# Input transposes ahead of the first modulation quarter, constant matmuls in TensorE's queue, and a low part behind the gating of the second channel half

## The reference

```python
mod_l = (silu(c) @ w_mod + b_mod)[:, None, :]          # w_mod: 1024 x 6144
sh1_l, s1_l, g1_l, sh2_l, s2_l, g2_l = jnp.split(mod_l, 6, axis=-1)
hl = modulate(rms_norm(xl, norm1_g), sh1_l, s1_l)      # h * (1 + scale) + shift
u = hl @ w_pw1 + b_pw1                                 # 1024 -> 2048
a, gate = jnp.split(u, 2, axis=-1)
u = a * jax.nn.sigmoid(gate)
u = dwconv(u.reshape(B * n_seg, L // n_seg, D), w_dw).reshape(B, L, D) + b_dw
u = jax.nn.silu(layer_norm(u, ln_g, ln_b))
yl = u @ w_pw2 + b_pw2
xl = xl + g1_l * yl
```

## Time and profile before

| | us |
|---|---|
| median of 3 runs (lowest, highest) | 1057.15 (1057.11, 1057.98) |
| the profiled execution | 1056.59 |
| its span | 1054.8 |
| TensorE busy | 1009.1 |
| VectorE busy | 604.5 |
| ScalarE busy | 512.8 |
| GpSimd busy | 24.2 |

### The profile page before, as it was taken

One profiled execution on the slowest core, in us unless ns is written; L12 is line 12 of the kernel. 1 busy time (PEld: TensorE's weight loads), 2 busy tenths in 40 slices (PEclk: granted clock), 3 DMA queues, 4 the chain that ended last, 5 costly groups with the idle time before them and its releaser, 6 DMA issues.

```text
span 1054.8 us, 13782 instructions
## 1 busy us (share of the span) xinstructions
PE 1009.1 (96%) x5788; PEld 854.1 (81%) x5788; DVE 604.5 (57%) x691; ACT 512.8 (49%) x643; POOL 24.2 (2%) x47
## 2 busy tenths in 40 slices
PE   5998999999998999899999999999998999999996
PEld 3665779999987999787888888889987788888885
DVE  3487455443558658756555545664886554554464
ACT  4444456445444547644443444654664544434453
POOL 0000000000000000000000000000000100000000
PEclk8999999999999999999999999999999999999998
DMA  9967587555515533055555555435322555555531
GB/s 353 410 232 278 234 348 274 202 189 195 192 51 204 183 142 121 2 180 204 203 185 180 194 199 204 164 133 190 121 80 81 190 199 196 176 186 199 179 121 40
DMA packets 30647, 195.56 MB, mean 185 GB/s; under 512 B 3571, under 2 KB 5672, under 8 KB 9592
## 3 DMA queue, kind: packets, MB, share of 16 engines
q1 hardware_dynamic: 30586, 194.68, 51.1%
HBM read 193.61 MB, written 2.04 MB: 185 GB/s over the span
## 4 chain that ended last, share of the span: by engine, by line
PE 80%; DVE 11%; ACT 4%; issue 3%; DMA 1%; POOL 0%; SPq 0%; DVEq 0%; POOLq 0%; ACTq 0%
PE ps L1527 56%; PE ps L1885 9%; PE ps L1938 4%; DVE lo L1006 3%; ACT hi L569 2%; PE ps L1623 2%; DVE scratch L1328 1%; DVE scratch L1144 1%; DMA raw<-stream 1%; PE ps L2164 1%; PE ps L2068 1%; PE ps L2022 1%; PE ps L2141 1%; PE ps L1640 1%; PE ps L1604 1%
## 5 line engine op out<-in xcount | busy, mean ns | idle before, releaser
L1006 DVE TENSOR_TENSOR lo<-raw,hi 128x2048 fp32r<-128x2048 f32 (+4 forms) x140 | 316.0, 2260 | 255.1 <-ACT hi L569 255.0
L569 ACT ACTIVATE hi<-raw 128x2048 fp32r<-128x2048 f32 (+4 forms) x140 | 263.9, 1888 | 135.7 <-PE ps L1527 114.7
L1527 PE MATMUL ps<-hi,xh 128*128 128x512 f32 (+2 forms) x704 | 275.3, 391 | 10.5 <-DVE lo L1006 5.8
L1527 PE MATMUL ps<-lo,xh 128*128 128x512 f32 (+2 forms) x704 | 269.1, 382 | 0.0
L1527 PE MATMUL ps<-hi,xl 128*128 128x512 f32 (+2 forms) x704 | 269.1, 382 | 0.0
L1527 PEld LDWEIGHTS ps<-hi,xh 128*128 128x128 f32 x704 | 132.3, 188 | 46.3 <-issue 12.6
L1527 PEld LDWEIGHTS ps<-lo,xh 128*128 128x128 f32 x704 | 132.3, 188 | 25.1
L1527 PEld LDWEIGHTS ps<-hi,xl 128*128 128x128 f32 x704 | 132.5, 188 | 22.6
L1527 PE MATMUL ps<-hi,gh 128*128 128x512 f32 (+2 forms) x328 | 125.1, 382 | 0.0
L1527 PE MATMUL ps<-lo,gh 128*128 128x512 f32 (+2 forms) x328 | 124.6, 380 | 0.0
L1527 PE MATMUL ps<-hi,gl 128*128 128x512 f32 (+2 forms) x328 | 124.6, 380 | 0.0
(11 more groups left out here) (251 smaller groups left out, 1083.1 us busy)
## 6 DMA issues: line engine op xcount, KB each, us to landing
raw<-stream SPq DMA_DIRECT2D x142, 1024.0 KB, 4.9
scratch<-stream SPq DMA_DIRECT2D x22, 1024.0 KB, 6.4
raw<-stream SPq DMA_DIRECT2D x4, 1020.0 KB, 4.9
raw<-stream SPq DMA_DIRECT2D x4, 896.0 KB, 5.0
raw<-stream SPq DMA_DIRECT2D x2, 864.0 KB, 5.1
raw<-stream SPq DMA_DIRECT2D x2, 768.0 KB, 4.6
raw<-stream SPq DMA_DIRECT2D x2, 680.0 KB, 5.2
h<-x SPq DMA_DIRECT2D x2, 512.0 KB, 4.2
```

What stands on the lines that cost most here:

```text
L569: nc.scalar.activation(hi[:, u["s"] % SPLIT_SLOTS, 0:n], raw_of(u, n), ACT.Copy).then_inc(S["hi_done"], 1)
L1006: nc.vector.tensor_tensor(lo[:, slot, 0:n], raw_of(u, n), hi[:, slot, 0:n].bitcast(F32), ALU.subtract).then_inc(S["lo_done"], 1)
L1527: ins = nc.tensor.matmul(out, l, r, start=start and i == 0, stop=stop and i == 2, skip_group_check=skip)
```

## The change

Three edits.

On TensorE the transposes of the input come first, then quarter 0, the bias products of pw1, then quarter 1 and the column sums; before, quarter 0 stood ahead of the transposes, and quarter 1 and the column sums ahead of the bias products. ScalarE follows: both copies to `xnT`, then the copy of quarter 0.

`keep_busy(times)` multiplies `neg_ones` by itself into bank 7, which nothing reads until it is overwritten: 14 times at the very start, behind `init_p` 3, and 7 times between the bias products and quarter 1 (`WARM`).

On VectorE the low part of pw2's second unit moves from ahead of `gated(1)` to behind the normalisation of block 1.

```diff
--- before.py
+++ after.py
@@ -174,6 +174,9 @@
 COLUMN_UNITS = ((0, 1), (2, 3), (4, 5), (6, 7), (12, 13), (14, 15), (16, 17), (18, 19))
 
 
+WARM = (14, 7)
+
+
 def copies(m):
 
     return m + 1 if m < SPLIT_ROWS[0] else m + 1 - len(SPLIT_ROWS)
@@ -653,11 +656,11 @@
                     nc.scalar.activation(sig[:, b, :], ps[:, 4 * c + 2 * b + 1, :], ACT.Sigmoid).then_inc(S["sig_done"], 1)
 
             squares(0)
-            quarter_copy(0)
             for b in range(NB):
                 act.wait_ge(S["xnT_ps"], b + 1)
                 nc.scalar.activation(xnT[:, :, b * P:(b + 1) * P], ps[:, 2 * b:2 * b + 2, :].rearrange("p a (k m) -> p (a k) m", k=4),
                                      ACT.Copy).then_inc(S["xnT_ready"], 1)
+            quarter_copy(0)
             feed(units_of(("pw1", 0))[0], 0)
             quarter_copy(1)
             group_high(0)
@@ -1160,7 +1163,6 @@
             dve.wait_ge(S["in_consts"], 32)
             for dst, c in ((ident16[:], C_ID), (masks16[:, 0, :], C_CAUSAL), (masks16[:, 1, :], C_STRICT)):
                 nc.vector.tensor_copy(dst, table[:, c:c + P]).then_inc(S["masks_done"], 1)
-            feed(units_of("pw2")[1], 0)
             gated(1)
             filtered(1, 0, 1, 2, 3)
             statistics(1, 0)
@@ -1173,6 +1175,7 @@
             dve.wait_ge(S["ln_rstd"], 2)
             nc.vector.tensor_scalar(xs[:, 1, :], ps[:, 2:4, :].rearrange("p a c -> p (a c)"), ln_mv[:, 1, 0:1], ln_rstd[:, 1:2],
                                     ALU.subtract, ALU.mult).then_inc(S["xc_ready1"], 1)
+            feed(units_of("pw2")[1], 0)
             columns(4)
 
             def low_pair(i, high, low):
@@ -1714,19 +1717,27 @@
                     ins = nc.tensor.transpose(ps[:, 4 + 2 * b + k // 4, (k % 4) * P:(k % 4 + 1) * P], xs[:, b, k * P:(k + 1) * P], ident)
                 ins.then_inc(S["xcT_ps"], 1)
 
-            pe.wait_ge(S["csb_done"], 1)
-            quarters(0)
+            def keep_busy(times):
+
+                for _ in range(times):
+                    nc.tensor.matmul(ps[:, 7, 0:P], neg_ones[:], neg_ones[:], start=True, stop=True)
+
+            pe.wait_ge(S["init_p"], 3)
+            keep_busy(WARM[0])
             pe.wait_ge(S["in_ident"], 16)
             for b in range(NB):
                 pe.wait_ge(S["xs_ready"], xsval(0, b))
                 for k in range(KT):
                     ins = nc.tensor.transpose(ps[:, 2 * b + k // 4, (k % 4) * P:(k % 4 + 1) * P], xs[:, b, k * P:(k + 1) * P], ident)
                 ins.then_inc(S["xnT_ps"], 1)
-            quarters(1)
-            column_sums(0)
+            pe.wait_ge(S["csb_done"], 1)
+            quarters(0)
             pe.wait_ge(S["pick_done"], 3)
             pe.wait_ge(S["xnT_ready"], NB)
             open_pw1(0)
+            keep_busy(WARM[1])
+            quarters(1)
+            column_sums(0)
             for i in range(GROUPS):
                 if i < GROUPS - 1:
```

## The result

| | before | changed |
|---|---|---|
| median of 8 runs each (lowest, highest) | 1057.76 (1057.11, 1061.93) | 1064.21 (1061.48, 1072.32) |
| ratio, 95% interval | | 1.0063 [1.0039, 1.0086] |
| the profiled execution | 1056.59 | 1068.28 |
| its span | 1054.8 | 1066.5 |

What follows compares the result with a forecast made beforehand. TensorE, busy 1009.1 of 1054.8 us, was taken as the bound, so only moving its queue earlier gains. Terms -3.25 - 1.9 + 4.2 + 2.2 = +1.25 on 1057.15 gave 1058.4 us, range 1055.6 to 1060.4.

Steps and rivals of the forecast that it cites:

- Term 1: Opening: quarter 3 starts at 22.95 instead of 26.20 us, held by its weight landing; -3.25 us.
- So no reordering on the engines moves it: Opening: unit 5, quarter 3's weights, lands at 22.82 us whatever the engines' order, the 16 DMA engines being full.
- 2.18 us of idle losing it before 18.54: Opening of the kernel before: TensorE's 2.18 us idle piece before 18.54 lost the full clock.
- a first product at 20: Opening: the first pw1 product starts at 19.9 us instead of 24.20, 4.3 us sooner.
- allows -3.3: Opening: quarter 5's weights, landing at 31.65 us and used at 35.05, leave room for a 3.3 us gain.
- Term 2: Gating: with the low part moved, filter products start at 89.89 instead of 91.77 us; -1.9 us.
- Term 3: Before quarter 15: unit 26's issue waits for the moved low part, so TensorE waits for the landing; +4.2 us.
- Rival (d): Before quarter 15: no wait for unit 26, because the slot comes free otherwise; -5.15 us, 1052.0 us, chance 0.07.
- Term 4: From quarter 15: the idle wait loses the full clock for 4.4 us, costing half; +2.2 us, bounds 0 and 3.3.
- nearer to the first: Behind the wait: low stretch taken as 4.4 us, nearer the first start's 4.2 to 5.2 than 6.6.
- Rival (e): Opening: gains nothing because every landing slips with the queue's order; +4.5 us, 1061.65 us, chance 0.04.
- Rival (c): Opening: clock lost between constants and input, quarter 3 at 24.4 us; sum +2.7 us, 1059.85 us, chance 0.10.

Runs made afterwards that it cites:

- e7: Changed kernel with the low part back ahead of the gating and units 7 to 9 issued only after unit 5's landing; one time, 1058.48 us.
- e13: The changed kernel profiled once more, nothing edited; 1062.54 us.
- e4: Changed kernel with 16 more constant matmuls on TensorE in the wait before quarter 15; 1063.83 us, ratio 1.0047 to before.
- e1: Changed kernel with only the low part of pw2's second unit back ahead of the gating, opening as changed; 1057.75 us, ratio 0.9990 to before.
- e3: Changed kernel with quarter 11 put ahead of pw2's second unit in the weight stream; 1058.31 us, ratio 1.0001 to before.
- experiment 4: Why quarter 3 came late: changed opening, low part back, with no constants, held issues or wide constants; quarter 3 at 24.18, 24.38 and 23.09 us.
- experiment 5: Changed kernel, low part back, with 10 more constants before quarter 3, to test the clock there; one time, 1065.90 us.
- e10: Changed kernel with the low part back and 9 constant matmuls of 512 columns for 21 of 128; 1058.58 us, ratio 0.9996 to before.
- e2: Kernel before with only the low part moved behind the normalisation of block 1, old opening; 1065.53 us, ratio 1.0056 to before.
- e8: Changed kernel with the low part back and 10 more constants on TensorE right before quarter 3; one time, 1065.90 us.
- e5: Changed kernel with the low part back and no constant matmuls at all; one time, 1055.64 us.
- e11: Changed kernel with 9 wide constants and quarter 11 ahead of pw2's second unit in the stream; 1058.39 us, ratio 0.9990 to before.

## Why the prediction was wrong

**Term 1 (-3.25): failed; it was 0.** In other executions with this opening it was hardly better or worse (q4 32.16 in e7, 32.57 in e13, 33.65 in e4, 34.25 in e1, 34.79 in e3, against 32.45 to 33.32 in four with the old one). Two steps of it failed. "So no reordering on the engines moves it" took the landing at 22.82 for a property of the stream alone. But the edit added instructions, and their fetch goes over the same 16 DMA engines: 24.42 (experiment 4). The working charged the 21 constants with TensorE's time only. And no price was put on the clock behind quarter 3: a wait of 2.86 us lost it for 3.4 us, though the text had 2.18 us of idle losing it before 18.54. The forecast of a first product at 20 left a hole before 22.95 of 1.4 us; grown to 2.9, it cost the rest (experiment 5). The side step that quarter 5 "allows -3.3" fell too: with quarter 3 mended, it allows 2.0 (e10), again by a late share.

**Term 2 (-1.9): right**, 2.2 at the filter products and 2.13 at quarter 14.

**Term 3 (+4.2): right.** Quarter 15 would have stood at 102.87 - 2.13 = 100.74 and stands at 104.89: +4.15. In place of the issue at 96.93 and landing at 101.83 the low part ended at 99.88 and the landing at about 104.75: both later by the 3 us that the opening didn't give, and apart by the same 4.9. Rival (d) is out: the wait is there in all four traces with the moved low part and the old order of units (changed twice, e2, and e4 under its constants), and gone with the new order (e3).

**Term 4 (+2.2, bounds 0 and 3.3): the mechanism right, the size not.** It is +4.0: 5.97 at the marker, less -2.13 and +4.15, leaves 3.95, and e4 measured 3.87 on its own. It isn't one size: from q15 to the marker it takes 8.03 us before, 11.98 and 12.05 in the two executions of the changed kernel, and 11.06 in e2, where the low stretch was 6.8 us and term 4 thus 3.0. The low stretch is 10.2 us, not 4.4, and 8.5 us of it have work in them. It holds the 5.42 us that 12 pw2 products took for 2.95, quarter 15 (1.94 for 1.07) and the bias products. The step that failed is "nearer to the first": low stretches of the opening, 4.2 to 6.6 us long, were taken as the bound for one in the middle of dense work.

**The sum.** 0 - 2.13 + 4.15 + 3.95 = +5.97, against the forecast's +1.25. Of the difference, 3.25 is term 1 and 1.8 is term 4; terms 2 and 3 gave 0.3 the other way. Rival (e), "the opening gains nothing, because every landing slips with the queue's order", had the outcome at 0.04 and nearly the number (1061.65), with the wrong cause: of the first six landings, units 0 to 3 are where they were (17.45 for unit 3 in both), and only units 4 and 5 slip. Rival (c), the clock lost between the constants and quarter 0, was not it in either execution of the changed kernel: quarter 0 took 1.07. But it is real: in e1 and e8, with the same opening, the transposes took 3.35 and 3.60 us for sixteen, with the clock at 1.2 GHz from 9.2 to 12.6 and from 8.4 to 11.9. The Trainium skill (TensorE: Matmul & The Clock Gate, Part 4: PE-mode transpose) says that the full clock does not engage for transposes. Here 1.06 us for a block of eight and the quarter behind them at full speed speak against it (the rows don't say whether they run in the mode that the page means), and so does e5, where nothing ran on TensorE before them:

```profile
8.58 3.45 PE L1731 MATMUL ps<-table,xs 128*128 128x128 f32 x16 [8.58 <-DVE xs L1063]
11.96 1.07 PE L1626 MATMUL ps<-raw,scratch 128*32 128x256 f32 x16
```

## What to carry to other kernels

Before a release (here a low part that frees a slot) is moved behind other work, look up which transfer waits for it and when that transfer's data is wanted; swapping two units in the stream kept the gain of the move and took away its whole loss. Instructions added to a queue cost their fetch as well, which competes with a saturated weight stream: to keep TensorE busy, few wide matmuls left the landing where it was and many narrow ones didn't (a difference of the traces, which the times don't resolve). An idle piece of TensorE of some 2 us or more is to be charged with the half-speed stretch that may follow, here as dear again as the wait itself.

## What the runs showed of the hardware

**Instruction fetches in the DMA engines.** Each is one 16 KB packet, 1.1 us on one engine; the changed kernel's fall at 18, 38 and 59 us, those of before at 31 and 49. One of them ahead of the landing of a 1 MB unit, with all engines full, goes with a landing 0.6 to 1.7 us later: one of its 16 shares comes 1.0 to 1.75 us behind the other fifteen (0.04 to 0.7 with the packet elsewhere), and the units behind it stay about 1.1 us late in that share.

**How long the clock stays low.** After an idle piece of 4.03 or 3.93 us before quarter 15 the low stretch was 10.2 us (both executions of the changed kernel), after 4.12 us (e2) 6.8 us, after 2.86 us (quarter 3) 3.4 us. Stretches of 3.4, 6.8, 10.2 and once 13.7 us (e3, 19.8 to 33.4) were seen. What decides between them wasn't found.

**The same wait, both ways.** The prediction has the 1.87 us before the filter products as a wait that keeps the clock. Of the seven traces with the low part ahead of the gating, where this wait is 1.86 to 1.88 us, three kept it (before, e5, e10) and four lost it for 3.4 us at 90 to 98 us (e1, e7, e8 and the second execution of before). The seven with the low part moved have no such wait and no low stretch there, which may be a gain of the move beyond its 2.1 us.

**The spread of the times.** The kernel before ran between 1054.71 and 1065.46 us in about 70 executions, and the time goes with the mean granted clock of the execution: 0.996 at 1055.0, 0.994 at 1057.1, 0.989 at 1060.2, 0.982 at 1065.0. The profiles show where it goes: short stretches at 1.2 GHz near 330, 424 to 462 and 790 to 820 us, in or just behind stages in which TensorE has small gaps (5.05 us busy of 6 in 424 to 430 before), present in one execution and absent in the next of the same kernel. In dense work such a stretch costs about half its length, so 1.7 us for the shortest and 5 for the longest, as much as the gains sought. Whether an earlier opening makes them more frequent, which would explain that e11's 3.66 us don't show in the medians, is left open: a profile is one execution, and 14 don't settle it.
